# Attention: the reciprocals of the softmax denominators spread over 64 partitions through memory in place of four transposes on the array

## What is computed

```python
# 8 query heads, 2 key/value heads, head dimension 64; 2048 queries, 256 + 2048 = 2304 keys, float32
qb = q.reshape(B, S // Q_BLOCK, Q_BLOCK, N_KV_HEADS, GROUP, HEAD_DIM).transpose(1, 0, 2, 3, 4, 5)
def one_block(qblk):
    s = jnp.einsum('bqkgd,bskd->bkgqs', qblk, k).astype(jnp.float32) * scale
    pr = jax.nn.softmax(s, axis=-1).astype(v.dtype)
    return jnp.einsum('bkgqs,bskd->bqkgd', pr, v)
```

## Time and profile before

| | |
|---|---|
| median of 3 runs | 2675.53 us (2673.7 to 2677.98) |
| the profiled execution | 2679.62 us, span 2677.8 us |
| PE, weight loads | 2486.5 us busy (93% of the span), 1711.3 (64%) |
| DVE, ACT, POOL | 1705.4 (64%), 1012.2 (38%), 700.3 (26%) |
| attention steps | about 1640 to 2400 us |
| mean granted TensorE clock | 0.965 |
| memory traffic | 164 GB/s over the span |

### The profile page before, as it was taken

How to read it: one execution, slowest core, us unless ns; L and a number is a source line. 1 busy time by engine, 2 the same in 40 slices (tenths; PEclk the granted TensorE clock), 3 DMA queues, 4 the chain that set the end, 5 groups by cost and what they waited for, 6 DMA issues and landing times. The chain is left out here.

```text
span 2677.8 us, 34539 instructions
## 1 busy us (share of the span) xinstructions
PE 2486.5 (93%) x11265; PEld 1711.3 (64%) x11265; DVE 1705.4 (64%) x2746; ACT 1012.2 (38%) x1766; POOL 700.3 (26%) x313
## 2 busy tenths in 40 slices
PE   4898899999999998999999968999998999978998
PEld 1576677777777776777777743555544455536776
DVE  3236564654556450879988876777777777775664
ACT  4144454444435330422222114445554445441222
POOL 0233211101101200102000005566677566640000
PEclk8999999999999998999999987999999999988999
DMA  7964788389478746488758553111121111004334
GB/s 271 350 204 143 244 281 285 141 279 321 172 244 281 271 163 240 165 307 299 255 196 270 190 167 90 30 29 30 27 58 55 30 29 25 25 24 163 129 134 156
DMA packets 225131, 453.44 MB, mean 169 GB/s; under 512 B 23957, under 2 KB 82571, under 8 KB 224756
## 3 DMA queue, kind: packets, MB, share of 16 engines
q1 hardware_dynamic: 193960, 351.04, 38.9%
q10 hardware_dynamic: 31052, 100.87, 11.0%
HBM read 328.86 MB, written 109.35 MB: 164 GB/s over the span
## 5 line engine op out<-in xcount | busy, mean ns | idle before, releaser
L2117 DVE TENSOR_REDUCE att_mx<-att_bank_m 128x1 f32<-128x512 f32 (+1 forms) x640 | 365.4, 630 | 125.7 <-PE att_bank_m L1926 125.7
L2066 ACT ACTIVATE att_p_f<-att_bank_s 128x512 f32<-128x512 f32 x576 | 316.8, 597 | 305.2 <-PE att_bank_s L1967 296.0
L1907 POOL TENSOR_TENSOR att_den<-att_den,att_p_f 128x1024 f32<-128x1024 f32 x160 | 379.6, 2373 | 60.1 <-ACT att_p_f L2066 49.2
L1618 DVE SCALAR_TENSOR_TENSOR proj_conv_acc<-proj_conv_in,proj_conv_w,proj_conv_acc 128x512 f32<-128x512 f32 (+1 forms) x480 | 337.4, 772 | 0.0
L562 PE MATMUL gla_bank_g<-mid_a_hi,mid_w_hi 128*128 128x512 f32 x768 | 311.6, 406 | 2.3 <-DMA mid_w_lo<-scratch_w_lo 1.1
L562 PE MATMUL gla_bank_g<-mid_a_hi,mid_w_lo 128*128 128x512 f32 x768 | 301.5, 393 | 0.0
L562 PE MATMUL gla_bank_g<-mid_a_lo,mid_w_hi 128*128 128x512 f32 x768 | 300.9, 392 | 0.0
L1941 PE MATMUL att_bank_o<-att_p_f,att_v 128*64 128x512 f32 x1152 | 269.0, 602 | 0.0
L562 PEld LDWEIGHTS gla_bank_g<-mid_a_hi,mid_w_hi 128*128 128x128 f32 x768 | 145.3, 189 | 49.2 <-issue 17.7
L1941 PEld LDWEIGHTS att_bank_o<-att_p_f,att_v 128*64 128x64 f32 x1152 | 74.3, 137 | 145.3 <-issue 96.7
L562 PEld LDWEIGHTS gla_bank_g<-mid_a_hi,mid_w_lo 128*128 128x128 f32 x768 | 145.1, 189 | 31.8
(11 more groups left out here) (404 smaller groups left out, 4803.1 us busy)
## 6 DMA issues: line engine op xcount, KB each, us to landing
mid_w_hi<-scratch_w_hi SPq DMA_DIRECT2D x100, 512.0 KB, 4.6
mid_w_lo<-scratch_w_lo SPq DMA_DIRECT2D x100, 512.0 KB, 6.1
mid_w_hi<-scratch_w_hi ACTq DMA_DIRECT2D x84, 512.0 KB, 3.9
mid_w_lo<-scratch_w_lo ACTq DMA_DIRECT2D x84, 512.0 KB, 5.0
scratch_w_hi<-mid_w_hi SPq DMA_DIRECT2D x54, 512.0 KB, 6.3
scratch_w_lo<-mid_w_lo SPq DMA_DIRECT2D x54, 512.0 KB, 7.2
mod_wslab<-in_ada_w SPq DMA_DIRECT2D x6, 2048.0 KB, 17.9
first_w_raw<-in_gla_w_in SPq DMA_DIRECT2D x24, 512.0 KB, 6.5
```

Source lines behind the costliest of these rows:

```text
L1618: dve.scalar_tensor_tensor(acc, src, conv_w[:, c, k:k + 1], acc, ALU.mult, ALU.add).then_inc(taps, 1)
L1907: pool.tensor_tensor(den[s][:], pair(0) if j == 1 else den[s][:], pair(j), ALU.add).then_inc(den_pool, 1)
L2066: act.activation(p_f[:, kt, :], S[kt % SBANKS][:], ACT.Exp, scale=float(HD) ** -0.5).then_inc(p_done, 1)
L2117: dve.reduce_max(mx[:, qt, n:n + 1], M[p % MBANKS][:, 0:min(TB, KEYS - TB * n)], AX_X).then_inc(mx_read, 1)
```

## The change

The reciprocals no longer go through PE. SP writes `recip` (128 partitions x 4 columns) to a row of 512 numbers in memory, waits for it, and loads that row into each of the 64 partitions of `o_out`. DVE's `finish` multiplies the sum of O by that in place, and stands in turn 14, behind `column`, instead of turn 5. The first `weigh` of a step waits for `recip_done` instead of `o_done`. `invert` waits for the store of `recip` and the store of `o_out` of the step before. The transfers stand in SP's program just ahead of the wait for `o_done`. After the last step SP does the same once more.

```diff
+                def spread_reciprocal(i):
+                    sp.wait_ge(recip_done, UP + i + 1)
+                    sp.dma_start(d["recip"].rearrange("o (t p) -> p (o t)", p=P), recip[:], allow_slow_non_contiguous=True).then_inc(recip_stored, 16)
+                    sp.wait_ge(recip_stored, UP + 16 * i + 16)
+                    sp.dma_start(o_out[:], d["recip"].broadcast_to([HD, TB])).then_inc(r_row, 16)
...
                     if before is not None:
+                        spread_reciprocal(i - 1)
                         sp.wait_ge(o_done, UP + i)
                         sp.dma_start(d["att"][ds(((i - 1) // NB) * HD, HD), ds(((i - 1) % NB) * TB, TB)], o_out[:]).then_inc(o_stored, 16)
                 steps(sp, body)
+                spread_reciprocal(STEPS - 1)
                 sp.wait_ge(o_done, UP + STEPS)
...
                     if j == 0:
-                        need(pe, o_done, i)
+                        need(pe, recip_done, i)
...
-                def spread_reciprocal(i):
-
-                    pe.wait_ge(recip_done, UP + i + 1)
-                    for qt in range(NT):
-                        last = pe.transpose(O[:, P * qt:P * (qt + 1)], recip[:, qt:qt + 1].broadcast_to([P, P]), ident[:])
-                    last.then_inc(r_row, 1)
...
-                        if kt == 7 and before is not None:
-                            spread_reciprocal(i - 1)
...
-                spread_reciprocal(STEPS - 1)
...
                 def invert(i):
                     dve.wait_ge(den_sum, UP + i + 1)
-                    need(dve, r_row, i)
+                    need(dve, recip_stored, 16 * i)
+                    need(dve, o_stored, 16 * i)
                     dve.reciprocal(recip[:], O[:, 0:NT]).then_inc(recip_done, 1)
 
                 def finish(i):
-                    dve.wait_ge(r_row, UP + i + 1)
+                    dve.wait_ge(r_row, UP + 16 * i + 16)
                     dve.wait_ge(o_sum, UP + i + 1)
-                    need(dve, o_stored, 16 * i)
-                    dve.tensor_tensor(o_out[:], o_hi[:], O[0:HD, :], ALU.mult).then_inc(o_done, 1)
+                    dve.tensor_tensor(o_out[:], o_hi[:], o_out[:], ALU.mult).then_inc(o_done, 1)
...
-                        if kt == 5 and before is not None:
-                            finish(i - 1)
...
                         if kt == 14 and after is not None:
                             column(i + 1)
+                        if kt == 14 and before is not None:
+                            finish(i - 1)
```

More of the change, by code:

```diff
@@ L1780, in attention @@
             sem(n) for n in ("s_done", "p_done", "den_pool", "den_dve", "pv_done"))
-        den_sum, o_hi_done, recip_done, r_row, o_sum, o_done, o_stored = (
-            sem(n) for n in ("den_sum", "o_hi_done", "recip_done", "r_row", "o_sum", "o_done", "o_stored"))
+        recip_stored, den_sum, o_hi_done, recip_done, r_row, o_sum, o_done, o_stored = (
+            sem(n) for n in ("recip_stored", "den_sum", "o_hi_done", "recip_done", "r_row", "o_sum", "o_done", "o_stored"))
         NC = 4
@@ L2492 @@
 SCRATCH = {"h1t": (D, SEQ), "qt": (512, SEQ), "kt": (P, KEYS), "vtok": (KEYS, P), "za": (512, SEQ), "zc": (512, SEQ),
-           "conv_y": (512, CONV_AT + SEQ), "att": (512, SEQ),
+           "conv_y": (512, CONV_AT + SEQ), "att": (512, SEQ), "recip": (1, TB),
            "w1_hi": (32, P, KT * P), "w1_lo": (32, P, KT * P),
```

## The result

| | before | after |
|---|---|---|
| median of the runs (lowest to highest) | 2676.03 us (2673.7 to 2677.98, 4 runs) | 2712.32 us (2708.46 to 2717.14, 4 runs) |
| profiled execution: span, granted clock | 2677.8 us, 0.965 | 2713.2 us, 0.952 |

The ratio is 1.0137 [1.0116, 1.0158]: 36 us slower, where no change was forecast. The same kernel was timed once more later, beside the experiments: 2701.10 us (2699.02 to 2704.64) against 2678.08, ratio 1.0082 [1.0057, 1.0107].

What follows compares the result with a forecast made beforehand. PE was taken to set the pace of steady steps; -8.8 there, +1.6 in steps 15 to 18, +0.2 in step 31 and +5.6 at the end gave -1.4, a median of 2674.1 us, range 2665.7 to 2683.

Steps and rivals of the forecast that it cites:

- PE's removal, 0.34 us a steady step: Transposes gone from PE save 0.44 us, less a wait for turn 6's exp: 0.34 in 26 steady steps, -8.8 us.
- Rival A: In the steps PE keeps the whole 0.44 us and the port costs nothing: -7.4, 2668 us; chance 0.27.
- finish at turn 14 is free in a steady step: On DVE, finish waits for POOL and takes about 1.9 us instead of 0.68, but idle time covers it: 0.
- Steps 15 to 18, +0.75 each: Where POOL has two more adds, finish delays the reductions PE awaits by 0.75 us; with the removal, +1.6 in all.
- The store, 4.5 us, between 2.3 and 7.4: SP's store of the reciprocals, 512 pieces of 4 bytes, taken at 4.5 us to landing, bounds 2.3 and 7.4.
- the load, 2.3 us taken: SP's load of the reciprocal row into 64 partitions, taken at 2.3 us.
- Hidden in every step: Inside steps, store and load together take 6.8 us (4.6 to 10.2), within 11.5 us before finish, so cost nothing.
- The end, +5.6: After the last step finish waits 6.8 us for the row instead of 1.21, uncovered: +5.6 us (3.4 to 9.0).
- rival D: At the end, the high end plus a store a microsecond over its bound: +6, 2681.5 us; chance 0.05.
- Step 31, +0.2: In the last step finish stands behind DVE's late convolution work, +0.62 against 0.44 of PE time: +0.2 us.
- Rival B: Row landing over 13.5 us after the reciprocal stalls steps; at 16 us, +75 and 9 at the end, 2758; chance 0.07.
- Rival C: The port costs in every steady step, say 0.4 us over in 26 steps: +10.4 more, 2684.5 us; chance 0.08.

Runs made afterwards that it cites:

- experiments 2 and 3: Changed kernel without its row transfers, finish at turn 14 multiplying by fixed values: in SBUF (2) 2693.37 us, in a PSUM bank (3) 2677.26 us.
- experiment 7: Changed kernel with POOL's first add of a step waiting for fold_den of the step before: 2704.19 us, ratio 1.0084.
- experiment 8: Kernel before with its transposes left out, finish still at turn 5, output not normalised: 2674.29 us, ratio 0.9982.
- experiments 4 and 6: Changed kernel, reciprocals stored as 128 pieces of 16 bytes (4), 2787.37 us, or from step 1 as 128 of 4 bytes (6), 2704.34 us.

## Why the prediction was wrong

By its own steps:

- *PE's removal, 0.34 us a steady step.* 0.25 (23.07 to 22.82). The wait for the exp of turn 6 is there, as foreseen, and takes 0.19 of the 0.44. Turn 9 of the step shown above:

```profile
1914.46 0.40 PE L1968 MATMUL att_bank_s<-att_q_b,end_k_b 65*128 65x512 f32 x1
1914.76 0.50 PE L1967 MATMUL att_bank_s<-att_q_a,end_k_a 128*128 128x512 f32 x1
1915.10 0.39 PE L1968 MATMUL att_bank_s<-att_q_b,end_k_b 65*128 65x512 f32 x1
...
1914.76 0.19 PEld L1967 LDWEIGHTS att_bank_s<-att_q_a,end_k_a 128*128 128x128 f32 x1 [0.33 <-ACT att_p_f L2064]
```

  The product starts 0.30 us after the one before and its partner 0.34 behind it, where 0.24 is usual: the refill that went with the transposes came back with the wait. The sum had counted the wait at 0.10 and the refill as gone. Mis-sized by 0.09, 2.3 us over 26 steps. Rival A (0.27), the whole 0.44, is out by the same figure.
- *finish at turn 14 is free in a steady step.* Right, also at the 1.9 us foreseen for it: experiments 2 and 3 have the same 22.82. In the changed kernel itself the row reads 0.68 us and not 1.9 in most steps, because it waited for the DMA until POOL was done. The Trainium skill's rule on the port (SBUF — State Buffer, "SBUF: two separate sides") was taken right there, and the trace agrees: 1.8 us against 0.68 with a PSUM operand.
- *Steps 15 to 18, +0.75 each.* **The first step that failed.** By the lengths used here these are steps 14 to 17, with step 18 as their tail. They cost 21 us more (19.8 and 1.2), not 1.6. The delay was followed from finish over POOL's two adds to the reductions, but not to the next operation with two SBUF inputs behind them: fold_den used to start 0.36 us before POOL's first add (2011.82 and 2012.18), the delay of finish used that up, and the lock cost 2.1 us more in each of four steps (experiment 7), and the clock went from 0.92 to 0.82. The price of the lock alone is 12.5 us here (experiments 2 and 3), with 3.7 more in steps 1 and 2, which the prediction took as steady; 3.0 of step 14 is one of the half-clock stretches that only the first measurement has. The sum also counted PE's removal as a gain of 0.34 in each of the four: by experiment 8 steps 14 to 18 take 4.6 us more for it.
- *The store, 4.5 us, between 2.3 and 7.4.* **The second.** 8.2 to 11.4 us, beyond the upper bound. It was bounded by pieces of 64 bytes and by the packets' own time. The packets behaved as foreseen, they were through in some 0.35 us (rows below), and then nothing is seen for 7.6 us until the completion. The nearest rows were not near: there is a step between pieces of 4 and of 16 bytes (experiments 4 and 6). The Trainium skill's bound of 512 B (DMA: Bandwidth & Descriptors, "Specifications") lies above both sizes and does not tell them apart.

```profile
DMA packets 528, 0.00 MB, mean 3 GB/s; under 512 B 528, under 2 KB 528, under 8 KB 528
...
q1 hardware_dynamic: 528, 0.00, 36.0%
```

  This is the window from 1914.5 to 1915.2 of the changed kernel, in which the whole store passed. The other miss in this term is the load, 2.3 us taken, 4.4 measured, though the loads of q of the same size are at 2.9. The upper bound of both together, 10.2, does not follow from its own terms either: 7.4 and 2.3 are 9.7. That half microsecond changes nothing.
- *Hidden in every step.* Wrong by this: 13.4 to 14.7 us against slack of 11.5 to 13.5. The slack itself was well read: a finish 14.5 us or more after the reciprocal made the next two steps 0.6 to 0.8 and 2.8 to 3.0 us longer than 22.82 (steps 24 and 25, 28 and 29), one at 14.2 to 14.3 the next by 0.3 or so, one below 13.9 none. The 2.8 to 3.0 are the half clock (0.62 from 2253 to 2262, in the first rows above).
- *The end, +5.6.* +12.5 (11.5 in the later measurement), over the 9.0 of the high end and what rival D (0.05) adds to it. The mechanism was right, nothing covers it; both transfers were mis-sized. With 16-byte pieces it is +3.7, inside the range given.
- *Step 31, +0.2.* -0.4, and step 30 -1.2. Small.

Rival B (0.07) came true in part: its threshold of 13.5 was passed by 1.2 us at most, in few steps by over 1, so it cost 12 us in the steps and not 75. Rival C (0.08) was right in kind and wrong in place: the port costs where POOL has extra work, not in the steady steps. The doubts were given as alternatives; in the event both came at once. Put together from the runs, the first measurement is: removal -3.4, place +0.6, port +16.1, late row +11.9, end +12.5, in all 37.7. The later one is the same with +0.2 for the late row and +11.5 for the end, 25.0, where the spans differ by 21.7 and the medians by 23.0. These are differences of single executions in a row, so they add up by their making; how far each could move is seen in the 11 us between two executions of one kernel.

## What to carry to other kernels

When an operation with two SBUF inputs is moved next to POOL's, follow the delay past the first wait to the next such operation: the lock is paid again wherever the order of two queues turns over, and it turned over on 0.3 us. Don't price a transfer of very small pieces by its packets or by larger pieces: a row spread by a store of 4-byte pieces costs 13 us round trip, one of 16-byte pieces 5, and either is free only with that much slack in every execution. And a saving on the engine that sets the pace (0.25 us a step) is lost in steps whose pace others set, which the clock can make dearer still. A transfer that fits its slack in one execution can miss it in the next, and here a microsecond more a step cost 12 us, 9 of them in three stretches at half clock.

## What the runs showed of the hardware

- A store of 4-byte pieces to memory completed 7.2 to 8.6 us (128 pieces, median 7.7) or 6.9 to 11.5 (512 pieces, medians of the executions 8.2 to 9.1) after its issue, one of 128 16-byte pieces after 1.4 by the median, though the packets of the 512 were through in 0.35 us.
- The load of one 2 KB row into 64 partitions took 3.3 to 4.4 us by the medians of the executions, that of 64 different rows 2.9.
- A weight load of 128x128 with a stride of 16 bytes took 327 ns by the mean instead of 198; DVE's 64x512 product with one operand read so takes 1.05 us instead of 0.67.
- The clock of steps 14 to 18 differs between kernels with nearly the same waits of PE: 0.92 and 0.88 with 1.4 to 1.6 and 0.70 us. It also fell to half for 10.2 us where both waits had been filled, and for 6.8 us behind waits of 0.25 us or less.
